# Two-layer block pair, gated recurrent unit: three down groups in its tail, taken block by block, and a new order of value projections and transposes behind it

## The reference, cut to what matters

```
def _rglru_mixer(h, w_in, conv_w, conv_b, w_a, b_a, w_x, b_x, lam, w_out):
    u, g = jnp.split(h @ w_in, 2, axis=-1)
    ...
    _, hs = lax.associative_scan(_lin_combine, (a, b_in), axis=1)
    y = hs.astype(h.dtype) * jax.nn.silu(g)
    return y @ w_out
...
    x = x + gate[:, None, :] * y            # end of the recurrent layer
...
    h = _modulate(_rmsnorm(x, kv_norm_g), shift, scale)
    k, v = jnp.split(h @ w_kv, 2, axis=-1)  # start of the attention layer
```

## Time and profile before

| | |
|---|---|
| median of 3 runs | 904.69 us (901.39 to 906.22) |
| span of the profiled execution | 905.0 us |
| PE busy in it | 824.7 us, 91% |
| DVE / ACT / POOL busy | 619.8 / 402.8 / 152.1 us |
| mean granted TensorE clock | 0.949 |

### The profile page before, as it was taken

The page is one execution under the profiler, slowest core; times in us unless marked ns, Lnnn a source line. Parts: engine busy times, 40 slices in busy tenths (PEclk is TensorE's granted clock), DMA queues, the critical chain, the costliest instruction groups (busy, mean ns, idle before and its releaser), DMA issues.

```text
span 905.0 us, 12983 instructions
## 1 busy us (share of the span) xinstructions
PE 824.7 (91%) x5338; PEld 754.1 (83%) x5338; DVE 619.8 (68%) x925; ACT 402.8 (45%) x469; POOL 152.1 (17%) x86
## 2 busy tenths in 40 slices
PE   6999799999999889999799999997888968979985
PEld 6999589999999687867799999995778958979974
DVE  6777667877787666665787777776477773546643
ACT  5442234444434044451444444343566873544631
POOL 0110122243431100000132243312200011030000
PEclk9999979999999999889799999998798988999999
DMA  7875248887776134432388867772044442744101
GB/s 292 335 279 185 95 150 300 318 332 264 265 263 253 66 118 150 153 131 77 134 314 298 337 268 262 268 261 93 24 163 146 191 152 94 279 140 140 47 24 47
DMA packets 25691, 174.38 MB, mean 193 GB/s; under 512 B 2848, under 2 KB 3104, under 8 KB 6176
## 3 DMA queue, kind: packets, MB, share of 16 engines
q1 hardware_dynamic: 25632, 173.54, 52.2%
HBM read 172.48 MB, written 1.05 MB: 192 GB/s over the span
## 4 chain that ended last, share of the span: by engine, by line
PE 80%; DVE 11%; ACT 5%; POOL 2%; issue 2%; DMA 0%; DVEq 0%; POOLq 0%; SPq 0%; ACTq 0%
PE bank L478 15%; PE bank L479 14%; PE bank L480 14%; PE Y L539 9%; PE Y L536 9%; PE Y L537 9%; DVE w_low L1125 2%; PE bank L502 1%; PE bank L561 1%; POOL small L787 1%; PE bank L503 1%; PE bank L504 1%; PE Y L597 1%; DVE small L1161 1%; DVE x L1189 1%
## 5 line engine op out<-in xcount | busy, mean ns | idle before, releaser
L1125 DVE TENSOR_TENSOR w_low<-raw,w_high 128x2048 fp32r<-128x2048 f32 (+2 forms) x130 | 286.1, 2223 | 65.4 <-ACT w_high L843 65.0
L478 PE MATMUL bank<-xT_h,w_high 128*128 128x256 f32 x1040 | 305.4, 294 | 17.1 <-DVE xT_l L1215 6.2
L479 PE MATMUL bank<-xT_l,w_high 128*128 128x256 f32 x1040 | 300.6, 289 | 0.0
L480 PE MATMUL bank<-xT_h,w_low 128*128 128x256 f32 x1040 | 300.4, 289 | 0.0
L843 ACT CAST w_high<-raw 128x2048 fp32r<-128x2048 f32 (+2 forms) x130 | 239.1, 1853 | 90.9 <-DMA raw<-weights 90.8
L478 PEld LDWEIGHTS bank<-xT_h,w_high 128*128 128x128 f32 x1040 | 206.3, 198 | 19.8 <-issue 12.3
L479 PEld LDWEIGHTS bank<-xT_l,w_high 128*128 128x128 f32 x1040 | 206.4, 198 | 0.4 <-issue 0.2
L480 PEld LDWEIGHTS bank<-xT_h,w_low 128*128 128x128 f32 x1040 | 206.0, 198 | 0.0
L536 PE MATMUL Y<-w_high,hT_h 128*128 128x512 f32 x344 | 135.1, 393 | 0.0
L537 PE MATMUL Y<-w_low,hT_h 128*128 128x512 f32 x344 | 134.3, 390 | 0.0
L539 PE MATMUL Y<-w_high,hT_l 128*128 128x512 f32 x344 | 107.1, 393 | 0.0
(11 more groups left out here) (182 smaller groups left out, 969.5 us busy)
## 6 DMA issues: line engine op xcount, KB each, us to landing
raw<-weights SPq DMA_DIRECT2D x152, 1024.0 KB, 5.3
rows<-rows_in SPq DMA_DIRECT2D x9, 512.0 KB, 7.1
raw<-weights SPq DMA_DIRECT2D x6, 768.0 KB, 4.3
raw<-weights SPq DMA_DIRECT2D x4, 512.0 KB, 4.6
x<-x_in SPq DMA_DIRECT2D x2, 512.0 KB, 4.2
out<-x SPq DMA_DIRECT2D x2, 512.0 KB, 2.6
consts<-consts_in SPq DMA_DIRECT2D x1, 320.0 KB, 5.3
cols<-cols_in SPq DMA_DIRECT2D x1, 118.5 KB, 6.5
```

The costliest lines, as they stand in the source:

```text
L478: mm(dst, high, xh[:, kt, :], start=kt == 0, stop=False)
L479: mm(dst, high, xl[:, kt, :], start=False, stop=False)
L480: last = mm(dst, low, xh[:, kt, :], start=False, stop=kt == kts - 1)
L1125: tt(w_low[:, n % RING, start:COLS[n]], slot[:, start:COLS[n]], f32(w_high[:, n % RING, start:COLS[n]]), ALU.subtract).then_inc(raw_done, 1)
```

## The change

The gated unit's tail now has three groups (1, 2 and 3) in place of one, and the loop of step 4 issues no down any more. Behind it, the transposes of a block are followed by both value halves of that block. On ACT the two copies of block 0's values stand ahead of the scaling of block 1's transposes. DVE's, POOL's and SP's instructions and the order of weight pieces stay as they are.

```diff
-TAIL = {"sc": 3, "ff0": 3, "mla": MXG, "ff1": 3, "rg": 1, "mo": MXG}
+TAIL = {"sc": 3, "ff0": 3, "mla": MXG, "ff1": 3, "rg": 3, "mo": MXG}
...
-    t.extend([("rs2kv", 0, 0), ("rs2kv", 0, 1), ("mo", "v", 0, 0), ("rs2kv", 1, 0), ("rs2kv", 1, 1)])
-    t.extend(("mo", "v", b, n) for b, n in ((0, 1), (1, 0), (1, 1)))
+    for b in range(TB):
+        t.extend([("rs2kv", b, 0), ("rs2kv", b, 1), ("mo", "v", b, 0), ("mo", "v", b, 1)])
...
-                for n in {MXG - 1: (0,), MXG: range(1, MXG - 1)}.get(g, ()):
+                if g == MXG - 1:
                     for b in range(TB):
-                        down("rg", n, b)
+                        down("rg", 0, b)
...
             tail("rg")
-            rs2kv_transposes(0)
-            moba_values(0, 0)
-            rs2kv_transposes(1)
-            moba_values(0, 1)
-            for n in range(2):
-                moba_values(1, n)
+            for b in range(TB):
+                rs2kv_transposes(b)
+                for n in range(2):
+                    moba_values(b, n)
...
                 scaled_transposed("rs2kv", b, *modulation["rs2kv"])
                 if b == 0:
                     rms_norm("rs2", "rg", 1)
-            for b in range(TB):
                 for n in range(2):
                     if b:
                         split_ahead(("mo", "v", 2 * n + 1))
```

## The result

The changed kernel is slower. Its median is 913.63 us (912.73 to 914.26, 4 runs) against 904.52 us, a ratio of 1.0090 (95% interval 1.0063 to 1.0117). Run again beside the kernel before on another occasion it had 911.63 us (6 runs) against 905.8 (17 runs), a ratio of 1.0071 (1.0048 to 1.0094). The forecast was slower, 909.8 us, with a range of 906.2 to 912.6: right in direction, and too small in size, with the first median outside the range and the second within it. (A ratio is estimated from the single runs, with its interval, and need not equal the quotient of the two medians: 1.0063 to 1.0117 stands for 5.7 to 10.6 us.)

The account below looks back on a forecast made before the run. PE was taken to bound the kernel, holding 80% of the last-ending chain, with no DMA on it. Holes +4.0 and clock +1.1 gave +5.1 us on the median 904.69: 909.8 us, range 906.2 to 912.6.

Parts of the forecast that it names:

- hole ahead of down 3 of block 0: PE waits for the last hidden values with only two downs ahead in place of four: a new 5.0 us.
- hole ahead of block 0's transposes: PE's old wait of 4.48 us for block 0's z closes, covered by three downs of block 1.
- hole behind them: PE waits behind block 0's transposes for DVE's queue, block 1's residual included: 6.3 us in place of 2.7.
- hole behind block 1's transposes: The third hole: PE waits for DVE's low part, 2.7 us, in place of 2.8 for ACT's copy.
- lost to the clock: PE slow behind the three holes: 2.44, 2.44 and 1.1 us, in sum 6.0 against 4.9 before.
- seam against the 56.6 of before: From down 1's first matmul to the first key product: holes +4.0 and clock +1.1, together +5.1 us.
- the value order: Values (0, 1) ahead of block 1's transposes: a hole of 2.7 us for one of 2.8.
- the costly rival: Clock falls after all three holes for as long as at the longest: 7.3 to 8.1 us lost, 911.1 to 911.9; chance 0.19.
- my four holes: Four earlier PE waits near 3 us, read as losing 0, 0, 2.7 and 1.56 us; mean 1.1 for the third hole.
- each such microsecond at the seam goes to the end of the program: Time lost at the seam passes unchanged to the end, since PE runs the key products without a wait from 776 us.
- slower 0.57: Chance of a time above the line at 909.2 us; the same had 0.37, faster 0.06.

Follow-up runs that it names:

- The experiments that take the change apart: Kernel before with the three-group tail alone: ratio 1.0085; kernel before with the new order of values, transposes and ACT's copies alone: 1.0006.
- the two on DVE's queue: Changed kernel with block 1's residual moved behind block 0's scaled transposes on DVE: 1.0015; with only value piece 1's low part moved there: 1.0034.
- The kernel with DVE's order mended: Changed kernel with block 1's residual moved behind block 0's scaled transposes on DVE: 906.54 us, ratio 1.0015.
- the one with 3.2 us more: Changed kernel with 27 more thrown-away matmuls, 3.2 us, inside the last value product: 915.23 us, ratio 1.0101.
- the two later delays: Kernel before with 15 or 66 more thrown-away matmuls in the last value product, 1.8 or 7.9 us: 909.32 us (1.0036) and 914.45 us (1.0096).

## Why the prediction was right in direction and short in size

**The seam was priced nearly right.** Prediction and profile, in us:

| | forecast | changed kernel | again |
|---|---|---|---|
| hole ahead of down 3 of block 0 | 5.0 | 4.9 | 6.4 |
| hole ahead of block 0's transposes | 0 | 0 | 0 |
| hole behind them | 6.3 | 6.1 | 6.1 |
| hole behind block 1's transposes | 2.7 | 2.7 | 2.7 |
| lost to the clock | 6.0 | 5.3 | 5.3 |
| seam against the 56.6 of before | +5.1 | +3.9 | +5.5 |

(The holes count from the moment at which the next matmul could have started; clock is the seam less 41.6 us of work at 2.4 GHz and the holes.) The experiments that take the change apart, and the two on DVE's queue, bear out the mechanisms: the hidden values' wait is uncovered, the cover of block 0's z is bought with DVE's in-order queue, and the value order is worth nothing that can be measured. In each hole the term was within 0.2 us, save the first, whose size hangs on how early PE comes.

**The clock in the seam: terms off both ways.** After each of the three holes PE ran slow, the third included, which the costly rival expected; but each slow stretch was shorter than the 5.6 us of the earlier trace rows. Windows of the changed kernel (busy us and count by engine, granted clock):

```profile
730.10:733.90 3.80, 3.73 (x10) 2.94 (x11) 2.31 (x2) 3.80 (x3) 0.00 (x0) 0.56 0.02 4
750.00:754.40 4.40, 4.39 (x20) 4.40 (x21) 4.37 (x3) 0.97 (x2) 3.25 (x2) 0.50 0.55 218
767.20:771.00 3.80, 3.73 (x20) 3.76 (x21) 2.70 (x2) 3.32 (x2) 0.00 (x0) 0.61 0.00 0
```

About 3.8, 4.4 and 3.8 us slow, 1.7 + 2.0 + 1.6 = 5.3 us lost. The third hole is a term that I sized wrong, 1.1 for 1.6, and by a misreading. I called the clock up behind the holes of 2.92 and 3.03 us because the next two matmuls had the full pace. A window tells more. In the trace of before, behind the one of 2.92:

```profile
677.70:683.00 5.30, 5.23 (x31) 5.24 (x32) 5.19 (x10) 1.82 (x2) 0.00 (x0) 0.68 0.61 212
```

The clock of 0.68 shows that it fell soon after; 31 matmuls took 5.23 us in place of 3.72, 1.5 lost. Over 339.3 to 345 it was 1.00, so only one of my four holes was free, and their mean would have been 1.4 us. The third hole of the changed kernel is of this kind: its first matmul took 0.36 us, and the window has 0.61. The Trainium skill, "TensorE: Matmul & The Clock Gate", section "HAM oscillation — how this bites in real kernels", tells of a kernel in which each burst behind a DMA wait of about 3 to 5 us starts cold. I had stretched that to all three holes, though the third, of 2.7 us, is shorter than the waits it describes. In this trace PE ran slow behind all three, behind the third not from the first matmul. The price that I had put on it, 7.3 to 8.1 us for the three, was too high: 5.3 were lost, nearer to my 6.0. The kernel with DVE's order mended lost 4.8 us in its seam, behind holes of 4.9, 2.6 and 2.7.

**The step that failed: "each such microsecond at the seam goes to the end of the program".** The miss of 3.8 us to 913.63 is made up of the seam, 1.2 less than forecast, the part behind it, 2.8 more, the base, 2.1 (see below), and 0.1 by which PE came later to down 1. I took what lies behind the key products as fixed and left half a microsecond in the range for it. It isn't. From the first key product on, the same instructions took 128.65 us in the trace of before, the least of all 14 profiles, and 131.46 in the changed kernel. Eleven profiles lie between 128.65 and 130.05, so part of the 2.8 us is the luck of the one trace on which I worked. Two places make this up. One is behind the hole at the first query product, 3.9 us long in every profile; the rows are of the changed kernel, then of the one before:

```profile
810.10:816.10 6.00, 5.95 (x29) 5.98 (x30) 2.94 (x2) 1.42 (x1) 4.43 (x4) 0.52 0.15 31
```

```profile
806.00:809.50 3.50, 3.35 (x17) 3.38 (x18) 2.46 (x3) 1.54 (x1) 3.50 (x4) 0.57 0.00 0
```

PE is slow for some 5.7 us in one and 2.7 in the other; from this product to the first output wait of the attention it is 28.5 us against 27.2. Of the other twelve profiles, with this part unchanged in all, five have 28.5, four 28.0 to 28.3 and three 27.3 to 27.5. The other is the last stretch, from the last such wait to the end. The same 130 matmuls are in it, first in the changed kernel, then in the one before:

```profile
870.30:911.80 41.50, 30.60 (x130) 24.07 (x130) 14.39 (x30) 7.76 (x20) 1.50 (x4) 0.87 0.10 39
```

```profile
865.00:905.00 40.00, 29.12 (x130) 22.85 (x130) 14.38 (x30) 7.76 (x20) 1.50 (x4) 0.95 0.11 40
```

DVE, ACT and POOL are busy for the same time to a hundredth; PE takes 1.5 us more at a clock of 0.87 against 0.95. So it is 41.5 us in both profiles of the changed kernel and in the one with 3.2 us more, and 40.0 to 40.1 in the eleven others.

The 1.5 us have one place. Some 6 us into the stretch PE waits 1.53 us for DVE's buf_a, in every profile. The windows that start 1.9 us after this wait's end are, of the changed kernel and then of the one before:

```profile
878.30:882.30 4.00, 4.00 (x16) 3.42 (x15) 1.61 (x4) 0.87 (x3) 0.00 (x0) 0.70 0.07 11
```

```profile
873.00:877.00 4.00, 4.00 (x21) 3.37 (x20) 1.61 (x4) 0.81 (x2) 0.00 (x0) 1.00 0.31 109
```

So a wait of only 1.5 us was followed by the lower clock in three profiles and left the clock up in the others.

That this comes from the clock is shown: no other engine's time differs and PE's does. That a delay alone can cost more than it lasts is shown by the medians for one size: 4.0 us of dead matmuls in the kernel before cost 6.5 us. What stays open is why the clock falls at this place in just these three profiles: the delay of 4.0 us reached the stretch at 870.99, within a microsecond of the changed kernel's 870.26, and took 40.0. For the runs without a profile it isn't known which of them had it.

**The base was off.** I put the sum on the median because the span of 905.0 and the median of 904.69 "agree within 0.3". They are not the same measure. In every run since, the time is 1.8 us longer than the span (913.58 for 911.8, 912.84 for 911.0, 910.59 for 908.8). By that, the profiled execution of before took about 906.8 us. With larger samples the kernel before has a median of 905.7 to 905.9 us (17 to 29 runs). On the occasion of the two later delays it was 904.43 (7 runs). Setting a sum that was read from an execution of 906.8 us on the median of 904.69 made the forecast 2.1 us too low; the sample of three runs is at most some 1 us of that. The chances: slower 0.57 was the case. The costly rival, at 911.1 to 911.9, came nearest to the two measured times, but by luck: it expected the excess in the seam's clock, where 5.3 us were lost and not its 7.3 to 8.1.

## What to carry to other kernels

When work is moved so that one engine is covered, write down what every in-order engine has queued ahead of the result that is wanted next: here a wait of 4.5 us ahead of the transposes was covered, another of 4.9 us for the hidden values was uncovered, and 3.4 us came on top behind the transposes, since a residual that wasn't urgent stood ahead of a scaling that was, and moving one line on DVE took that last part back. A bank that is waited for can come free by moving its copy ahead of work whose operands come later, which gave 0.45% with no other change. And a delay need not cost what it lasts: near waits of 1.5 us and more, leave a margin of 1 to 3 us for the clock, also behind the place of the change, and don't take one profile's lucky stretch as the base.

## What the runs showed of the hardware

- The same instructions behind holes of the same length run slow for different times. After the hole of 3.9 us at the first query product, the slow stretch was 2.7 to 5.7 us over 14 profiles.
- A hole of 2.96 us put TensorE's clock down in one execution (0.56 from 697 to 704 us) and left it up in another (1.00), with no difference in the program up to there. In the 14 profiles this hole was 2.93 to 2.98 us long, and the clock over the 4 us behind it was 1.00 in seven and 0.50 to 0.64 in the seven others. In the last stretch a wait of 1.53 us was followed by the lower clock in three of 14. And the level may fall some matmuls behind a hole, so that their first rows mislead.
- Executions of one kernel spread by up to 10 us, mostly with the mean granted clock: of 29 of the kernel before on one occasion, the four at 0.960 to 0.964 took 898.1 to 903.3 us, the 25 at 0.949 to 0.956 took 902.4 to 907.7. (On another, one at 0.908 took 905.6.)
- POOL's small power step (L786, one value per partition) took 0.57 us while DVE was idle and 2.48 us beside DVE's splits, in the same execution of the changed kernel:

```profile
739.00 0.57 POOL L786 TENSOR_TENSOR small<-small 128x1 f32<-128x1 f32 x1
751.07 1.95 POOL L785 TENSOR_SCALAR small<-small 128x1 f32<-128x1 f32 x1 [11.49 <-ACT z L867]
753.10 2.48 POOL L786 TENSOR_TENSOR small<-small 128x1 f32<-128x1 f32 x1
```
